# The end of a mixture-of-experts step: result rows of five token tiles gathered in two parts around the last three expert steps, and the last step's gate weights loaded ahead of its up weights

## Chip, cores and metric

One core of one Trainium2 chip. The metric is the device time of one execution in microseconds (us); the kernel before was timed three times. One further execution of it was profiled, and all rows below are from that one.

## What is computed

One decoder layer over 1024 prompt tokens and 32 sample tokens: a gated merge of latent attention and a spatial-gating MLP, then a mixture of 64 SwiGLU experts of which each token takes two, then a last norm. All data are float32. The change is in the end of the mixture and in the last norm:

```python
def run_block(args):
    xb, e = args
    h = jax.nn.silu(xb @ w_gate[e]) * (xb @ w_up[e])     # 1024 -> 256, twice
    return h @ w_down[e]                                  # 256 -> 1024
...
out = ys[pos] * w_sorted[:, None].astype(ys.dtype)
return jnp.zeros_like(xt).at[tok_sorted].add(out.astype(xt.dtype))
...
return x + y.reshape(b, s, d)          # channel_mixer
...
y_prompt = rmsnorm(xp, norm_f_g)       # over all 1024 + 32 rows
y_sample = rmsnorm(xs, norm_f_g)
```

So a token's output row is norm(x2 + g0 * y(first expert) + g1 * y(second expert)).

## The kernel before

Five engines run programs of their own and meet at semaphores. SP only issues DMAs; POOL issues the indirect ones. Tokens are in NT = 9 tiles of 128 rows (the last has 32). The core's memory is one tensor, `arena`, cut by hand into regions that are used again from stage to stage.

**Expert steps.** Experts are ranked by load. The 8 fullest get a step each (up to 128 rows), the others go in pairs (64 rows each), 36 steps (NST) in all; `expert_steps` writes the order out. The last three steps hold the six experts of ranks 54 to 59, all pairs. Rank r's expert number is a value that is loaded from `order_i`. Its three matrices of 1 MB go into one of four slots `w_e[0..3]`, each with a gate, an up and a down part; the last step uses slots 2 and 3, the one before it slots 0 and 1. In step n:

- POOL: `rows_in` gathers the step's token rows from `xt_rows` into `xg[n % 4]`, up to six steps ahead (L1755).
- PE: `turn_rows(n + 1)` (L1254), `turn_hidden(n - 1)` (L1273), `gate_up(n)` (L1266), `down(n - 1)` (L1285). `gate_up` waits for the gate and up weights of all its slots before its first matmul.
- ACT and DVE: copies between PSUM and `arena`; DVE's part of the result row is L2228, its share of the turned rows L2215.
- POOL: `rows_out` copies an index (L1749) and scatters the result rows into the DRAM tensor `y_rows` (L1763), at row 2 * token + choice. `scattered` waits until a scatter has landed.
- SP: `w_load(slot, e, (0, 1))` issues gate, up, gate, up for step n as soon as gate_up of the slot's last user is done; then `down_load` of step n - 1 (all L719).
- DVE has some 30 small pieces of other work, `overflow(k)`, one group per step, that find experts with too many rows. If there are any, a loop runs more steps after the last. In the profiled execution it runs none.

**The end.** When all scatters have landed POOL raises `moe_end`. Then SP loads each tile's 2 x 1024 values per token from `y_rows` (1 MB a tile, L786) into `y2[t]`, nine loads in order, the last three held back by the use of four semaphores. `y_rows` has the two rows of a token next to each other, so this is one plain copy for each tile. Tiles in PE_TILES = (2, 4, 6) are combined on PE: three matmuls for each half row, by the identity on x2 and by the diagonals `diag[t][c]` of the gates on the two result rows (L1319 to L1321). The six other tiles are combined on DVE by two instructions (L2278, L2279). ACT then squares and sums each row (L1588) and takes the root (L1589), DVE inverts it (L2270) and scales (L2272), and SP stores the row (L778). DVE and ACT take the tiles in order 0 to 8; in DVE's program the scale of tile t - 2 follows the combine of tile t.

Of the kernel before, what the change touches and what calls it, by code (L numbers as in the profile page):

```python
# [29 lines left out]
P = 128  # L30
# [34 lines left out]
PE_TILES = (2, 4, 6)  # L65
# [156 lines left out]
def build(nc, x_prompt, x_sample, cache_ckv, cache_krope, page_table, norm1_g, w_in, q_norm_g, kv_norm_g,  # L222
# [4 lines left out]
    with ExitStack() as ctx:  # L227
# [204 lines left out]
        o = [attn_base]  # L432
        y2 = [take(2 * D, o) for _ in range(NT)]
        fin = [x[:, 0:D] for x in y2]
        junk8 = take(D, o)
        stat8 = [take(2, o) for _ in range(NT)]
        diag = {t: [take(P, o) for _ in range(2)] for t in PE_TILES}
# [62 lines left out]
        moe_end = sem("experts_done")  # L500
        f_in = [sem(f"y_rows_in{i}") for i in range(4)]
# [35 lines left out]
        def group_moves(what, n, out):  # L537
# [27 lines left out]
            return [(qsr[half, :].rearrange("p (b h t) -> p h b t", b=NB, h=H), src) for half in (slice(0, DR), slice(DR, P))]  # L565

# [14 lines left out]
        def _(sp):  # L581
# [169 lines left out]
            for n, (_, mine) in enumerate(steps):  # L751
# [3 lines left out]
                for (_, slot, use), e in zip(mine, e_of):  # L755
                    sp.wait_ge(e_gu, step_of[slot, use - 1] + 1)
                    w_load(slot, e, (0, 1))
# [8 lines left out]
            with sp.If(total > 0):  # L766
                with sp.Fori(0, NOVP) as j:
                    with sp.If(total > 2 * j):
# [3 lines left out]
                        w_load(0, e0)  # L772
                        w_load(1, e1)
# [7 lines left out]
            yr = y_rows.rearrange("(n c) d -> n (c d)", c=2)  # L781
            for t in range(NT):
                r = rows_of(t)
                if t >= 4:
                    sp.wait_ge(f_in[t % 4], 16 * (t // 4))
                sp.dma_start(y2[t][0:r, :], yr[t * P:t * P + r, :]).then_inc(f_in[t % 4], 16)  # L786
                if t >= 6:
                    out_rows(sp, t - 6)
            for t in range(3, NT):
                out_rows(sp, t)  # L790
# [4 lines left out]
        def _(pe):  # L795
# [461 lines left out]
            def gate_up(n, u, mine):  # L1257

                pe.wait_ge(e_xe, 2 * n + 2)
                for _, slot, use in mine:  # L1260
                    pe.wait_ge(e_w[slot], 32 * use)
                for x in range(2):
                    for k in range(KD):
# [39 lines left out]
            with pe.If(total > 0):  # L1303
                with pe.Fori(0, NOVP) as j:
                    with pe.If(total > 2 * j):
                        extra = [(None, s, j + loads[s] + 1) for s in range(2)]
# [8 lines left out]
            for k, t in enumerate(PE_TILES):  # L1315
                pe.wait_ge(f_in[t % 4], 16 * (t // 4 + 1))
# [276 lines left out]
        def _(pool):  # L1593
# [177 lines left out]
            row_of = [row for row, _ in steps]  # L1771
            for n in range(4):
                rows_in(n, row_of[n], n)
# [3 lines left out]
            k = 6  # L1777
            for n in range(NST):
                if n >= 2:
# [26 lines left out]
            pool.sem_inc(moe_end, 1)  # L1806

# [3 lines left out]
        def _(dve):  # L1811
# [357 lines left out]
            def overflow(k):  # L2169
# [37 lines left out]
                elif k == 9:  # L2207
                    tt(g_sub, logits[:, :, 0:NG], g_top[:, :, 0:1].broadcast_to([P, NT, NG]), ALU.subtract)
                    step(tt(d_sub, e_top[:, :, 1], e_top[:, :, 0], ALU.subtract))
                    dve.sem_inc(r_sub, 1)  # L2210

# [49 lines left out]
            dve.wait_ge(moe_end, 1)  # L2261
# [3 lines left out]
            last.then_inc(r_dve, 1)  # L2265

# [7 lines left out]
            for t in range(NT):  # L2274
                r = rows_of(t)
                if t not in PE_TILES:
                    dve.wait_ge(f_in[t % 4], 16 * (t // 4 + 1))
# [37 lines left out]
```

## Time and profile before

| | us |
|---|---|
| median of 3 runs | 2040.82 |
| lowest, highest | 2031.3, 2046.83 |
| profiled execution | 2023.4 |
| its span, first to last instruction | 2021.6 |

The profiled execution lies below the three timed ones. PE is busy 1857.5 us of the span and its mean granted clock is 0.959 of full speed. The expert steps take the time from about 1460 to 1983, the end from there.

### The profile page before, as it was taken

The page shows a single profiled execution, that of the slowest core. Times are in us where ns is not written, and L with a number is a line of the kernel's source. Part 1 is how long each engine was busy: PE and PEld are TensorE (multiplying, and loading weights), DVE is VectorE, ACT ScalarE, POOL GpSimd, SP SyncE. Part 2 cuts the span into 40 slices and gives each one's busy share as a digit, 9 for nine tenths or more (in the row PEclk, how much of TensorE's full clock was granted, in tenths as well). Part 3 has the DMA queues.
Part 4 walks back from the last instruction along what each step waited for, and adds up shares of the span by engine and source line. Part 5 has one row for each costly group of instructions (what it writes and reads, how often), then busy time and mean ns, then how long its engine had stood idle before and what let it go on. Part 6 is the DMA issues. An engine that isn't in the chain of part 4 may idle for free. (4 is left out here: it accounts for less than half of the span.)

```text
span 2021.6 us, 26766 instructions
## 1 busy us (share of the span) xinstructions
PE 1857.5 (92%) x10622; PEld 1088.8 (54%) x10622; DVE 598.3 (30%) x1385; ACT 426.5 (21%) x904; POOL 301.4 (15%) x428
## 2 busy tenths in 40 slices
PE   7999999999999999998999998999598988888884
PEld 5644444444445656565666664555365555555551
DVE  3110000022203334333555554555322211111116
ACT  3211111100002223332444333222110011101103
POOL 1021221111100000000111112243412111111100
PEclk9999999999999999998999998999598889999997
DMA  7212211378820000024999996454599999999986
GB/s 232 107 68 80 75 36 70 116 261 284 276 86 1 1 1 1 1 63 128 292 305 292 294 304 224 148 185 162 192 400 421 420 416 416 415 402 403 407 342 260
DMA packets 105267, 433.86 MB, mean 215 GB/s; under 512 B 24208, under 2 KB 29808, under 8 KB 74384
## 3 DMA queue, kind: packets, MB, share of 16 engines
q1 hardware_dynamic: 84880, 331.06, 43.5%
q0 software_dynamic: 20160, 101.24, 15.0%
q8 instruction: 68, 1.11, 0.2%
q14 instruction: 31, 0.25, 0.0%
q10 hardware_dynamic: 128, 0.20, 0.0%
HBM read 389.22 MB, written 63.66 MB: 224 GB/s over the span
## 5 line engine op out<-in xcount | busy, mean ns | idle before, releaser
L838 PE MATMUL psum<-arena 128*128 128x512 f32 (+1 forms) x1280 | 527.3, 567 | 0.0
L838 PEld LDWEIGHTS psum<-arena 128*128 128x128 f32 x1280 | 239.6, 190 | 259.7 <-issue 235.7
L1266 PE MATMUL psum<-arena 128*64 128x256 f32 (+1 forms) x2048 | 284.4, 411 | 66.4 <-DMA arena<-in_w_up_dram 65.5
L1266 PEld LDWEIGHTS psum<-arena 128*64 128x64 f32 (+1 forms) x2048 | 204.8, 155 | 136.2 <-issue 79.2
L1285 PE MATMUL psum<-arena 128*64 128x512 f32 (+1 forms) x512 | 131.4, 595 | 0.7 <-DVE arena L2223 0.7
L1896 DVE COPY arena<-psum 128x512 f32<-128x512 f32 (+5 forms) x52 | 27.8, 545 | 346.9 <-PE psum L883 194.0
L1033 PEld LDWEIGHTS psum<-arena 128*128 128x128 f32 x1024 | 112.7, 141 | 30.0 <-issue 28.0
L1435 ACT ACTIVATE arena<-psum 128x512 f32<-128x512 f32 (+1 forms) x72 | 40.5, 562 | 412.6 <-PE psum L838 400.0
L1033 PE MATMUL psum<-arena 128*128 128x128 f32 x1024 | 126.6, 276 | 0.3 <-DVE arena L1950 0.3
L1163 PE MATMUL psum<-arena 128*128 128x512 f32 x256 | 113.4, 600 | 1.3 <-ACT arena L1484 1.3
L2219 DVE TENSOR_TENSOR arena<-arena,psum 128x256 f32<-128x256 f32 x36 | 15.2, 422 | 321.4 <-ACT arena L1549 321.4
L1449 ACT COPY arena<-psum 128x512 f32<-128x512 f32 x128 | 71.8, 587 | 172.6 <-PE psum L1033 172.6
L1763 POOL DMA_INDIRECT y_rows<-arena x36 | 40.7, 1132 | 411.8 <-DVE arena L2228 393.9
L1044 PE MATMUL psum<-arena 128*32 128x512 f32 (+1 forms) x768 | 95.6, 611 | 1.5 <-DVE arena L1950 1.5
L1950 DVE COPY arena<-psum 128x512 f32<-128x512 f32 x128 | 87.7, 691 | 28.1 <-PE psum L1033 24.8
L1549 ACT ACTIVATE arena<-psum 128x256 f32<-128x256 f32 x36 | 13.8, 384 | 337.2 <-PE psum L1266 337.2
L1918 DVE STREAM_TRANSPOSE arena<-arena 128x512 f32<-128x512 f32 x64 | 41.8, 692 | 133.3 <-DMA rope_turned<-arena 104.9
L1285 PEld LDWEIGHTS psum<-arena 128*64 128x64 f32 (+1 forms) x512 | 45.5, 142 | 66.2 <-issue 63.2
L1163 PEld LDWEIGHTS psum<-arena 128*128 128x128 f32 x256 | 48.3, 192 | 60.2 <-issue 60.1
L932 PE MATMUL psum<-arena 128*128 128x512 f32 (+3 forms) x192 | 72.8, 502 | 3.0 <-ACT arena L1379 3.0
L958 PE MATMUL psum<-arena 128*128 128x128 f32 x576 | 72.1, 277 | 3.2 <-ACT arena L1407 1.5
L958 PEld LDWEIGHTS psum<-arena 128*128 128x128 f32 x576 | 68.8, 193 | 11.5 <-issue 6.2
(307 smaller groups left out, 1949.8 us busy)
## 6 DMA issues: line engine op xcount, KB each, us to landing
arena<-in_w_gate_dram SPq DMA_DIRECT2D x64, 1024.0 KB, 13.3
arena<-in_w_up_dram SPq DMA_DIRECT2D x64, 1024.0 KB, 20.1
arena<-in_w_down_dram SPq DMA_DIRECT2D x64, 1024.0 KB, 21.8
arena<-in_w_in_dram SPq DMA_DIRECT2D x8, 2048.0 KB, 8.2
z_act<-arena SPq DMA_DIRECT2D x64, 256.0 KB
rope_turned<-arena SPq DMA_DIRECT2D x32, 512.0 KB
arena<-rope_turned SPq DMA_DIRECT2D x64, 256.0 KB
arena<-z_act SPq DMA_DIRECT2D x8, 2048.0 KB, 10.1
```

The lines of the kernel that those rows point to most:

```text
L838: last = mm(out[:, 0:w], xn_t[:, k, t * P:t * P + P], w_blk[n % 2][:, k, 0:w], start=(k == 0), stop=(k == KD - 1))
L932: mm(outs[h], q_pair[p % 2][:, h, t * P:t * P + P], kv_pair[p % 2][:, h, c0:c0 + w], start=True, stop=False)
L958: last = mm(out[:, DV * h:DV * h + DV], prob_t[h][:, j, :], v_pair[p % 2][:, j, DV * h:DV * h + DV], start=(j == 0), stop=(j == t))
L1033: last = tr(bank(u % 4)[:, P * kk:P * kk + P], ck[q][:, key_row(j, kk), P * c:P * c + P], ident)
L1044: last = mm(bank(5)[RS * j:RS * j + RS, :], q_now[:, c, :] if c < 2 else qr_now[half, :], ck_t[:, c, j, :] if c < 2 else rope[:, 4 * j:4 * ...
L1163: last = mm(bank(4 + half), m_t[:, k, :], w_o_sb[:, k, 512 * half:512 * half + 512], start=(k == 0), stop=(k == KD - 1))
L1266: last = mm(bank(2 + u)[rows, DE * x:DE * x + DE], xg_t[u][:, k, rows], w_e[slot][x][:, k, :], start=(k == 0), stop=(k == KD - 1))
L1285: last = mm(bank(5 + half)[rows, :], h_t[:, f, rows], w_e[slot][2][:, f, 512 * half:512 * half + 512], start=(f == 0), stop=(f == 1))
L1449: nc.scalar.copy(turned_at(u), bank(u % 4)).then_inc(kt_in[0], 1)
L1763: pool.indirect_dma_start(y_rows, bass.IndirectOffsetOnAxis(ap=idx_row[s], axis=0), yo[s], None, bounds_check=last_slot, oob_is_err=False) ...
L1918: last = V.transpose(kr_b[n % 2][:, c, :].rearrange("p (r k) -> p r k", r=PG), kr_raw[n % 2][:, :, 32 * c:32 * c + 32])
L1950: copy(turned_at(u), bank(u % 4)).then_inc(kt_in[1], 1)
```

## The change

The tiles are split into EARLY_TILES = (1, 3, 5, 6, 7) and PLAIN_TILES = (0, 2, 4, 8), and PE_TILES becomes (1, 3, 5, 7).

- For an early tile POOL gathers the rows of `y_rows` by index, 128 rows by 1024 for each of the two choices. It does so twice, ten indirect DMAs each time. The first time it takes the rows whose experts ran before the last three steps; these ten stand behind `rows_out` of the third-last step. The second time, after `moe_end`, it takes the remaining rows. An index out of bounds skips its row.
- DVE works the two index lists out, in `overflow(10)` to `overflow(14)`.
- `y2[1], y2[3], y2[5], y2[7]` take the places of the gate and up parts of slots 0 and 1, `y2[6]` that of `xg[2]` and `xg[3]`. The overflow loop uses slots 2 and 3 in place of 0 and 1.
- `y_rows` is filled with the input rows x before, by four DRAM to DRAM copies of 8.65 MB in all, behind SP's stores of the new cache rows.
- SP loads only the four plain tiles after `moe_end`.
- In the last step SP issues gate, gate, up, up, and `gate_up` waits for the gates (on the semaphore `x_loaded[0]`), and before its up half for the ups.
- The diagonals are computed before the wait for `moe_end`; there are eight in place of six.

```diff
-PE_TILES = (2, 4, 6)
+PE_TILES = (1, 3, 5, 7)
+EARLY_TILES = (1, 3, 5, 6, 7)
+PLAIN_TILES = (0, 2, 4, 8)
+LATE_STEPS = 3
...
+        def y_there(eng, t):
+
+            if t in PLAIN_TILES:
+                eng.wait_ge(f_in[PLAIN_TILES.index(t)], 16)
+            else:
+                k = EARLY_TILES.index(t)
+                eng.wait_ge(c_in[k % 4], cache_moves(k % 4) + 32 * (k // 4 + 1))
...
+            sp.wait_ge(fill_in, 16)
+            for c in range(2):
+                sp.dma_start(y_rows[TOK * c:TOK * c + SEQ, :], xp).then_inc(fill_in, 16)
+                sp.dma_start(y_rows[TOK * c + SEQ:TOK * c + TOK, :], xs).then_inc(fill_in, 16)
...
+            def gates_first(mine, e_of):
+
+                for x, done in ((0, x_loaded[0]), (1, None)):
+                    for (_, slot, use), e in zip(mine, e_of):
+                        if x == 0:
+                            sp.wait_ge(e_gu, step_of[slot, use - 1] + 1)
+                        sp.dma_start(w_e[slot][x].rearrange("p k n -> p (k n)"),
+                                     (w_gate, w_up)[x][0, bass.ds(e, 1)].rearrange("e (p k) n -> p (e k n)", p=P)
+                                     ).then_inc(done or e_w[slot], 16)
...
-            for t in range(NT):
-                r = rows_of(t)
-                if t >= 4:
-                    sp.wait_ge(f_in[t % 4], 16 * (t // 4))
-                sp.dma_start(y2[t][0:r, :], yr[t * P:t * P + r, :]).then_inc(f_in[t % 4], 16)
+            for k, t in enumerate(PLAIN_TILES):
+                r = rows_of(t)
+                sp.dma_start(y2[t][0:r, :], yr[t * P:t * P + r, :]).then_inc(f_in[k], 16)
...
+                split = isinstance(n, int) and n == NST - 1
+                if split:
+                    pe.wait_ge(x_loaded[0], 16 * ((NT + 1) // 2) + 32)
...
                 for x in range(2):
+                    if split and x == 1:
+                        for _, slot, use in mine:
+                            pe.wait_ge(e_w[slot], 32 * use - 16)
...
+            def y_gather(t, c, rows_i, done):
+                m = 2 * t + c
+                pool.indirect_dma_start(y2[t][:, D * c:D * c + D], None, y_rows, bass.IndirectOffsetOnAxis(ap=rows_i[:, m:m + 1], axis=0),
+                                        bounds_check=last_slot, oob_is_err=False).then_inc(done, 16)
+
+            n_late = NST - LATE_STEPS
             for n in range(NST):
-                if n >= 2:
+                if 2 <= n and n - 2 != n_late - 1:
                     scattered((n - 2) % 4, (n - 2) // 4 + 1)
                 rows_out(n % 4, n, row_of[n], k)
...
+                if n == n_late:
+                    scattered((n_late - 1) % 4, (n_late - 1) // 4 + 1)
+                    pool.wait_ge(e_gu, NST - 1)
+                    pool.wait_ge(e_xt, NST)
+                    pool.wait_ge(rows_split, 1)
+                    for t in EARLY_TILES:
+                        for c in range(2):
+                            y_gather(t, c, early_i, e_x[1])
...
             pool.sem_inc(moe_end, 1)
+            pool.wait_ge(e_x[1], 16 * len([n for n in range(NST) if n % 4 == 1]) + 32 * len(EARLY_TILES))
+            for k, t in enumerate(EARLY_TILES):
+                if k >= 4:
+                    pool.wait_ge(c_in[k % 4], cache_moves(k % 4) + 32 * (k // 4))
+                for c in range(2):
+                    y_gather(t, c, late_i, c_in[k % 4])
...
-            dve.wait_ge(moe_end, 1)
             for t in PE_TILES:
                 for c in range(2):
                     last = ts(diag[t][c], ident, gates[:, t, c:c + 1], None, ALU.mult)
             last.then_inc(r_dve, 1)
+            dve.wait_ge(moe_end, 1)
```

POOL's program before, from the scatter of step 32 (the first L1763 here) to the first instruction behind the steps:

```order
L1763 DMA y_rows<-arena 2112x1024
L1749 COPY arena<-arena 128x1
L1763 DMA y_rows<-arena 2112x1024
L1749 COPY arena<-arena 128x1
L1763 DMA y_rows<-arena 2112x1024
L1749 COPY arena<-arena 128x1
L1763 DMA y_rows<-arena 2112x1024
L1789 TENSOR_LOAD arena
```

The same stretch after; L1810 is the scatter and L1828 the gather from `y_rows`:

```order
L1810 DMA y_rows<-arena 2112x1024
L1796 COPY arena<-arena 128x1
L1810 DMA y_rows<-arena 2112x1024
L1828 DMA arena<-y_rows,arena 128x1024 x10
L1796 COPY arena<-arena 128x1
L1810 DMA y_rows<-arena 2112x1024
L1796 COPY arena<-arena 128x1
L1810 DMA y_rows<-arena 2112x1024
L1851 TENSOR_LOAD arena
```

Ten gathers now stand between the scatter of step 33 and that of step 34; ten more end POOL's program.

SP's program before, from the last step's gate and up weights to the last down weights:

```order
L719 DMA arena<-in_w_gate_dram 128x2048
L719 DMA arena<-in_w_up_dram 128x2048
L719 ISA
L719 DMA arena<-in_w_gate_dram 128x2048
L719 DMA arena<-in_w_up_dram 128x2048
L719 DMA arena<-in_w_down_dram 128x2048 x4
```

And after:

```order
L753 DMA arena<-in_w_gate_dram 128x2048
L753 ISA
L753 DMA arena<-in_w_gate_dram 128x2048
L753 DMA arena<-in_w_up_dram 128x2048 x2
L760 DMA arena<-in_w_down_dram 128x2048 x4
```

The second gate load has moved ahead of the first up load; the down loads stay where they were.

DVE's program before, from the first combine to the scale of tile 2 (L2278 and L2279 combine, L2270 and L2272 scale; a scale that reads psum is of a PE tile):

```order
L2278 SCALAR_TENSOR_TENSOR arena<-arena 128x1024
L2279 SCALAR_TENSOR_TENSOR arena<-arena 128x1024
L2278 SCALAR_TENSOR_TENSOR arena<-arena 128x1024
L2279 SCALAR_TENSOR_TENSOR arena<-arena 128x1024
L2270 RECIPROCAL arena<-arena 128x1
L2272 SCALAR_TENSOR_TENSOR arena<-arena 128x1024
L2278 SCALAR_TENSOR_TENSOR arena<-arena 128x1024
L2279 SCALAR_TENSOR_TENSOR arena<-arena 128x1024
L2270 RECIPROCAL arena<-arena 128x1
L2272 SCALAR_TENSOR_TENSOR arena<-arena 128x1024
L2270 RECIPROCAL arena<-arena 128x1
L2272 SCALAR_TENSOR_TENSOR arena<-psum,arena 128x1024
```

And after, from the first combine to the combine of tile 4:

```order
L2370 SCALAR_TENSOR_TENSOR arena<-arena 128x1024
L2371 SCALAR_TENSOR_TENSOR arena<-arena 128x1024
L2370 SCALAR_TENSOR_TENSOR arena<-arena 128x1024
L2371 SCALAR_TENSOR_TENSOR arena<-arena 128x1024
L2362 RECIPROCAL arena<-arena 128x1
L2364 SCALAR_TENSOR_TENSOR arena<-arena 128x1024
L2362 RECIPROCAL arena<-arena 128x1
L2364 SCALAR_TENSOR_TENSOR arena<-psum,arena 128x1024
L2370 SCALAR_TENSOR_TENSOR arena<-arena 128x1024
L2371 SCALAR_TENSOR_TENSOR arena<-arena 128x1024
```

Before, three combines and two scales of DVE's own tiles stand ahead of the first scale of a PE tile; now two combines and one scale do.

## Rows read from the trace of the kernel before

**Rows 1.** The chain that ended last, 1860 to 2022: start us, us, what.

```profile
1939.33 22.95 DMA arena<-in_w_up_dram
...
1962.41 7.15 PE psum L1266 x64
...
1974.11 3.68 PE psum L1285 x16
...
1979.40 2.38 DMA y_rows<-arena
...
1983.77 9.21 DMA arena<-y_rows
```

**Rows 2.** Stretches: us, busy of PE, PEld, DVE, ACT, POOL; PEclk, DMA share, GB/s.

```profile
1956.00:1960.00 4.00, 4.00 (x24) 1.52 (x20) 0.42 (x1) 0.97 (x2) 0.00 (x0) 1.00 0.45 188
1962.00:1967.00 5.00, 4.59 (x43) 3.66 (x45) 0.00 (x0) 0.00 (x0) 1.05 (x2) 1.00 0.97 394
1967.00:1979.00 12.00, 10.09 (x58) 4.42 (x54) 2.14 (x4) 3.20 (x6) 1.17 (x2) 1.00 0.07 25
```

**Rows 3.** SP's queue in order of time: start us, us, line, what.

```profile
1960.29 0.81 SPq L719 DMA_DIRECT2D arena<-in_w_down_dram  x2
...
1982.92 10.41 SPq L786 DMA_DIRECT2D arena<-y_rows  x7
```

**Rows 4.** DVE in order of time, the end; in brackets the idle time before.

```profile
1982.99 1.27 DVE L2264 TENSOR_SCALAR arena<-arena 128x128 f32<-128x128 f32 x6 [2.86 <-POOLq L1806]
1988.04 1.29 DVE L2278 SCALAR_TENSOR_TENSOR arena<-arena 128x1024 f32<-128x1024 f32 x1 [3.78 <-DMA arena<-y_rows]
...
1990.56 1.28 DVE L2278 SCALAR_TENSOR_TENSOR arena<-arena 128x1024 f32<-128x1024 f32 x1
...
2001.89 0.17 DVE L2270 RECIPROCAL arena<-arena 128x1 f32<-128x1 f32 x1 [2.40 <-ACT arena L1589]
...
2005.81 0.15 DVE L2270 RECIPROCAL arena<-arena 128x1 f32<-128x1 f32 x1
...
2007.20 0.16 DVE L2270 RECIPROCAL arena<-arena 128x1 f32<-128x1 f32 x1
...
2017.96 1.27 DVE L2272 SCALAR_TENSOR_TENSOR arena<-arena 32x1024 f32<-32x1024 f32 x1
```

**Rows 5.** PE in order of time, the three tiles that it combines.

```profile
1993.12 2.04 PE L1319 MATMUL psum<-arena 128*128 128x512 f32 x2 [15.35 <-DMA arena<-y_rows]
...
2000.22 1.02 PE L1319 MATMUL psum<-arena 128*128 128x512 f32 x2
...
2005.37 1.02 PE L1319 MATMUL psum<-arena 128*128 128x512 f32 x2
```

**Rows 6.** POOL in order of time: scatters back to back, then single ones.

```profile
1429.52 0.98 POOL L1711 DMA_INDIRECT slot_rows<-arena  x1 [0.30 <-issue]
1430.81 0.98 POOL L1711 DMA_INDIRECT slot_rows<-arena  x1 [0.30 <-issue]
...
1548.74 2.32 POOL L1763 DMA_INDIRECT y_rows<-arena  x1 [13.74 <-DVE arena L2228]
...
1560.60 1.03 POOL L1763 DMA_INDIRECT y_rows<-arena  x1 [7.31 <-DVE arena L2228]
...
1961.88 0.98 POOL L1763 DMA_INDIRECT y_rows<-arena  x1 [17.92 <-DVE arena L2228]
...
1974.62 0.98 POOL L1763 DMA_INDIRECT y_rows<-arena  x1 [11.56 <-DVE arena L2228]
```

**Rows 7.** DVE at the same times as the two single scatters of Rows 6.

```profile
1547.75 2.42 DVE L2187 TENSOR_TENSOR arena<-arena 128x2176 f32<-128x2176 f32 x1
...
1559.60 2.41 DVE L2189 TENSOR_REDUCE arena<-arena 128x34 f32<-128x2176 f32 x1
```

**Rows 8.** Landing of the row gathers (L1755) from 1850 on.

```profile
DMA to landing us min/median/max: 8.5/8.7/8.9
```

**Rows 9.** Busy time in the stretch behind SP's stores of the cache rows.

```profile
650.00:850.00 200.00, 194.37 (x950) 119.95 (x949) 74.60 (x197) 61.14 (x138) 0.00 (x0) 1.00 0.00 1
```

More of the change, by code:

```diff
@@ L430, in build @@
         fill = w_uk_t.rearrange("p h c -> p (h c)")[:, 0:2 * NE * CAPR // P]
-        o = [attn_base]
-        y2 = [take(2 * D, o) for _ in range(NT)]
+        slot_at = [attn_base + 6 * D * s for s in range(4)]
+        y_home = {1: slot_at[0], 3: slot_at[0] + 2 * D, 5: slot_at[1], 7: slot_at[1] + 2 * D, 6: attn_base + 26 * D,
+                  0: slot_at[0] + 4 * D, 2: slot_at[1] + 4 * D, 4: slot_at[2], 8: slot_at[2] + 2 * D}
+        y2 = [take(2 * D, [y_home[t]]) for t in range(NT)]
         fin = [x[:, 0:D] for x in y2]
+        o = [slot_at[3]]
         junk8 = take(D, o)
         stat8 = [take(2, o) for _ in range(NT)]
-        diag = {t: [take(P, o) for _ in range(2)] for t in PE_TILES}
+        assert o[0] <= attn_base + 4 * 6144
+        o = [gains_base + 4 * D]
+        kept_in = take(2 * NT * NE, o).rearrange("p (m e) -> p m e", e=NE)
+        limit, is_late, row_f, row_at = (take(2 * NT, o) for _ in range(4))
+        early_i, late_i = (take(2 * NT, o).bitcast(U32) for _ in range(2))
+        assert o[0] <= free[0]
+        diag = {t: [kept_in.rearrange("p m e -> p (m e)")[:, 2 * P * k + P * c:2 * P * k + P * c + P] for c in range(2)]
+                for k, t in enumerate(PE_TILES)}
         assert o[0] <= attn_base + 4 * 6144
@@ L754, in _ @@
                 e_of = [sp.value_load(order_i[0:1, r:r + 1], min_val=0, max_val=NE - 1) for r, _, _ in mine]
-                for (_, slot, use), e in zip(mine, e_of):
-                    sp.wait_ge(e_gu, step_of[slot, use - 1] + 1)
-                    w_load(slot, e, (0, 1))
+                if n == NST - 1:
+                    gates_first(mine, e_of)
+                else:
+                    for (_, slot, use), e in zip(mine, e_of):
+                        sp.wait_ge(e_gu, step_of[slot, use - 1] + 1)
+                        w_load(slot, e, (0, 1))
                 if e_last:
@@ L1305, in _ @@
                     with pe.If(total > 2 * j):
-                        extra = [(None, s, j + loads[s] + 1) for s in range(2)]
+                        extra = [(None, s, j + loads[s] + 1) for s in (2, 3)]
                         turn_rows(NST + j, 0, xg_used + 1 + j)
@@ L2210, in overflow @@
                     dve.sem_inc(r_sub, 1)
+                elif k == 10:
+                    late_e = [r for _, mine in steps[NST - LATE_STEPS:] for r, _, _ in mine]
+                    assert late_e == list(range(late_e[0], late_e[-1] + 1))
+                    cap, used, past = cnt[1], cnt[2], cnt[3]
+                    ts(cap, placed, float(NBIG), float(BLK), ALU.is_lt, ALU.mult)
+                    ts(used, placed, float(late_e[0]), None, ALU.is_lt)
+                    step(ts(past, placed, float(late_e[-1] + 1), None, ALU.is_ge))
+                    step(tt(used, used, past, ALU.add))
+                    step(stt(cap, cap, float(BLK), used, ALU.add, ALU.mult))
+                elif k == 11:
+                    step(tt(kept_in, iota.unsqueeze(1).broadcast_to([P, 2 * NT, NE]), wide(e_f.rearrange("p t c -> p (t c)"), NE), ALU.is_equal))
+                elif k == 12:
+                    step(tt(kept_in, kept_in, cnt[1].unsqueeze(1).broadcast_to([P, 2 * NT, NE]), ALU.mult))
+                elif k == 13:
+                    step(red(limit, kept_in, AX.X, ALU.add))
+                elif k == 14:
+                    tt(is_late, rk.rearrange("p t c -> p (t c)"), limit, ALU.is_ge)
+                    step(copy(row_f, ids_sb.rearrange("p (n c) -> p n c", c=2)[:, :, 0]))
+                    step(stt(row_at, is_late, float(1 << 20), row_f, ALU.mult, ALU.add))
+                    step(copy(early_i, row_at))
+                    step(ts(is_late, is_late, -float(1 << 20), float(1 << 20), ALU.mult, ALU.add))
+                    step(tt(row_at, is_late, row_f, ALU.add))
+                    step(copy(late_i, row_at))
+                    dve.sem_inc(rows_split, 1)
             def rows_t(n, u):
```

20 lines of the change are left out of this document (11 added, 9 removed).

## Prediction

> **What bounds the kernel now.** I read the chain that ended last first, since the change only touches the end. From 1860 to 1962 us the chain is the weight stream: the last up weights are issued at 1939.33 and land 22.95 us later, at 1962.28 [rows 1]. Behind that point come, one after another: the last gate_up (7.15 us), the down matmuls of step 34, the hidden rows, the last down matmuls at 1974.11, the last scatter at 1979.40 which lands in 2.38 us, `moe_end`, SP's first load of result rows at 1982.92 [rows 3], the third of these (tile 2, 9.21 us to landing), and then PE from 1993.12 [rows 5]. The view by stretches shows what the change wants to use: from 1967 to 1979 the DMA engines are 7% busy at 25 GB/s [rows 2], while after `moe_end` 8.65 MB must be read and 4.3 MB stored. All that the change can touch lies between 1960 and 2021.6, some 60 us or 3% of the span, and most of that is work that stays.
>
> The end itself runs at DVE's pace. The reader should see in [rows 4] one idle time of weight, 2.40 us before 2001.89: DVE waits for the first tile that PE combines. PE starts at 1993.12, takes 7.1 us for that tile and 5.15 us for the next [rows 5], and ACT needs another 1.5 us until DVE can scale at 2001.89. From there DVE never stands still: seven scales and three combines. A scale costs 1.39 us (2005.81 to 2007.20), a combine 2.5 us (1988.04 to 1990.56). 7 x 1.39 + 3 x 2.5 = 17.2, so the sum gives 2019.1; the row says 2017.96 + 1.27 = 2019.2. The last store then takes 2.4 us to the end of the span. So before, **end = S + 8.8 + 17.2 + 2.4**, where S is PE's first combining matmul.
>
> **Gates ahead of ups.** Four loads of 1 MB come in the order gate, gate, up, up; at some 0.4 MB/us the two ups are 5 us of the stream, so the gates are there near 1957. PE had finished the down matmuls of step 33 by 1960.29, when SP issues the down loads that wait for them [rows 3], and stood still until 1962.41 but for two transposes. Now it can begin at about 1960.7; the gate half takes 3.6 us, and at 1964.3 the ups (1962.28) are there. Gain for the last down matmuls: 1.7 us, so the last result rows are in memory at about 1976.9 in place of 1978.6.
>
> **Ten early gathers on POOL.** The scatter of step 33 ends at 1962.86 [rows 6]. Back-to-back indirect DMAs are issued every 1.29 us [rows 6], so ten take 12.9 us, from 1963.1 to 1976.0. Queued behind them on POOL are the scatters of steps 34 and 35. An index copy and its wait cost 1.0 us each time (a scatter follows 1.0 us behind the end of the last DMA), so scatter 34 goes at 1977.0 (before 1974.62) and scatter 35 at 1979.0 (before 1979.40). POOL's queue is now what ends last there, not PE: of the 1.7 us of the gates 0.4 are left. Two things can take them back. The eight diagonals (8 x 0.21 = 1.7 us of DVE, from [rows 4]) now run at just that time; before they filled a wait. And the early gathers bring up to 5.2 MB into the DMA queue that the scatters use: at the 394 GB/s of [rows 2], with the 1.5 MB of down weights that are left at 1963.4, they drain by about 1980. Scatter 35 lands in 2.4 us if the queue is empty, in up to 5 us if not. I take `moe_end` at the same time as before, with bounds of -1 and +4 us. The last down weights, landed by 1967 before, share the DMA engines with the gathers; they would have to be 5 us late to be missed at 1972.4.
>
> **What is loaded after `moe_end`.** SP issues 3.25 MB in four loads, not 8.65 MB. Tile 0 comes as before (1988.04), tile 2 as the second load at about 1990.5, so DVE has no wait in front. For tile 1 POOL must issue two gathers, the second at 1984.2. Few rows are in them, so only the latency counts: 2.4 us as the last scatter [rows 1], 8.7 us as the row gathers under the weight stream [rows 8]. With SP's loads in flight until about 1991 I take 6.3 us: **S = 1990.5**, between 1986.6 and 1992.9; before it was 1993.12. The other four early tiles follow at 2.6 us each, by 1994.5 issued, ahead of PE's 5.15 us a tile.
>
> The latency under load is weighed against a rule: the Trainium skill (DMA: Bandwidth & Descriptors, Queues, rings and completion order) says that a DMA engine changes between queues only at packets of about 9 to 17 descriptors. That would explain the 8.7 us of [rows 8] and speaks for a value near it here; by it the sum would be 2 us higher.
>
> **DVE and PE at the end.** DVE has five combines in place of six and nine scales as before. Tile 1 is now PE's, and its scale is third in DVE's order, behind two combines and one scale, which are done by 1994.5. So DVE waits from there until S + 8.8 = 1999.3; then eight scales and three combines are left: 11.1 + 7.5 = 18.6. **End = S + 8.8 + 18.6 + 2.4 = S + 29.8 = 2020.3.** PE's four tiles end at S + 7.1 + 3 x 5.15 = S + 22.6, and their last scale stands at S + 24.7 in DVE's order: just covered. So PE starting 2.6 us earlier is paid back by one more scale behind the wait (1.4 us). Against the 2021.6 us of the span this is -1.3 us.
>
> **Edits with no cost.** The fill of `y_rows` (8.65 MB read and written) is issued near 605 us; from 650 to 850 the DMA engines move 1 GB/s [rows 9], and 17.3 MB need 88 us at half of the 394 GB/s of [rows 2]. The index work on DVE is two instructions of 1152 columns, a reduction and some fifteen small ones, some 7 us over five steps; DVE has pieces of 2.4 us in such steps already [rows 7], and between its copy of a result row and its next due copy lie some 7 us of gate_up. If that cover were gone it would be 7 us at most.
>
> **Rivals.** (1) *The late gathers come quickly.* S = 1986.6 and `moe_end` 1 us early: 2016.4 - 1 = about 2015.5, -6 us. For it: few bytes. Against: the 8.7 us of [rows 8].
>
> (2) *DVE keeps POOL from issuing the late gathers.* At 1548.74 a scatter took 2.32 us: it ended 0.9 us after a DVE TENSOR_TENSOR on two `arena` operands (1547.75 + 2.42); under a TENSOR_REDUCE of the same length the next took 1.03 us [rows 6, 7]. DVE's instructions at the end read two `arena` operands too, back to back from 1988 on. Four of the ten gathers are out by then. If each of the other six must wait for the end of a DVE instruction and 0.9 us more, they come every 2.5 us, the last at 2003, in time for PE. If POOL gets its turn only when DVE is idle, DVE's wait for tile 1 (4.8 us) serves three, and DVE then stands still at tile 6 for the rest: three issues and a landing, 3 x 1.29 + 3 = 7 us. That gives 2027, 6 us slower than before. It decides from the point at which late gathers take over 2.3 us each. The Trainium skill (SBUF — State Buffer, Who interferes with whom) says that a DVE instruction with two inputs in this memory contends with a GpSimd instruction that reads it, and that a reduction doesn't; the trace agrees.
>
> (3) *The early gathers hold up the last scatters and down weights.* 5.2 MB in one queue ahead of them, with DMA engines that finish unevenly: before, the stream was down to 45% from 1956 to 1960 [rows 2] while the last up weights still took until 1962.28. Such 4 us on `moe_end` give 2024.3, with a late tile 1 as well 2026.5: 3 to 5 us slower than before.
>
> **The numbers.** Forecast, within 3 us of 2020.3: 0.40. Rival 1: 0.20. Rival 2: 0.20. Rival 3: 0.20. The profiled execution took 2023.4 us, its span 2021.6; the median of three is 17 us higher, and the three differ by 15 us, which nothing in the end of the kernel explains. I carry the difference over: 2040.8 - 1.3 = 2039.5. The cases span -6 to +6 us; medians of so few runs can differ by some 7 us by themselves. Together the range is 2029 to 2050. No case reaches 1% (20 us, about what a measurement of this kernel can tell from no change): 0.03 faster, 0.93 same, 0.04 slower.
>
> **What would show it.** PE's last gate_up starts near 1960.7 and the scatter of step 35 is issued near 1979.0, behind ten gathers 1.29 us apart; `moe_end` is unchanged; PE's first combining matmul comes 7 to 8 us after SP's first load; DVE has one wait of 4 to 5 us before the first scale that reads PSUM. I am wrong if scatter 35 lands after 1985, if late gathers take over 1.3 us, or if a stretch before 1960 us gets longer.

## The result: half a per cent slower, and the profile after

| | before | after |
|---|---|---|
| median, us (20 runs each, same chip) | 2030.4 | 2040.01 |
| lowest, highest | 2024.11, 2046.83 | 2032.17, 2048.87 |
| ratio after/before, 95% interval | | 1.0046 [1.0033, 1.0059] |
| span of the profiled execution | 2021.6 | 2030.3 |

The change costs some 9 us. That is inside the 1% that I called "same", but its sign is not the one I forecast (-1.3 us). The absolute time, 2040.01, fell on my 2039.5 by luck, for a reason that has nothing to do with the change: the median of the three runs that I started from lies 10 us above the median of all twenty. From 2030.4 the same sum gives 2029.1, and the range of 2029 to 2050 is right only by this.

How to compare two profiles of this kernel needs one remark. The expert steps end at another time in each execution: SP's issue of the last two down loads, which falls on DVE's copy of the result row of step 33 (1960.29 in [rows 3]), is seen anywhere from 1956.9 to 1975.4 us in the twelve profiles. All that the change touches at the end comes behind that moment, so I count from it ("+13.8" is 13.8 us behind it).

The changed kernel was profiled twice, and the first profile holds a disturbance that none of the ten later profiles shows: at 1970 and at 1976 it has waits of ACT (12.80 us) and DVE (4.92 us) that end 4 to 6 us behind the matmuls they wait for, with a releaser that the trace doesn't know. Its cause stays open, and I read the second profile (`e5_again`, the same kernel, span 2037.1) for the time up to `moe_end`. Behind `moe_end` the two agree within 0.7 us.

PE of the second profile, which answers to the first rows of [rows 1] and to [rows 5]; columns start, us, what, and in brackets the idle time before it and what ended it:

```profile
1968.13 7.17 PE L1313 MATMUL psum<-arena 128*64 128x256 f32 x64
1975.89 3.66 PE L1332 MATMUL psum<-arena 128*64 128x512 f32 x16 [0.58 <-DMA arena<-in_w_down_dram]
1979.48 0.51 PE L1320 MATMUL psum<-arena 128*128 128x128 f32 x2
1982.85 5.35 PE L1332 MATMUL psum<-arena 128*64 128x512 f32 x16 [2.87 <-DMA arena<-in_w_down_dram]
2007.26 2.05 PE L1366 MATMUL psum<-arena 128*128 128x512 f32 x2 [19.05 <-DMA arena<-y_rows,arena]
```

The zero point of this profile is 1967.80. gate_up of the last step starts at +0.3 (before +2.1, [rows 1]). But the last down matmuls start at +15.05 instead of +13.82, because now they wait for their weights, and they take 5.35 us instead of 3.68. The stretches say why they take longer:

```profile
1968.00:1976.00 8.00, 7.42 (x68) 4.68 (x69) 1.07 (x3) 0.38 (x1) 5.09 (x6) 1.00 0.92 338
1976.00:1980.00 4.00, 3.98 (x18) 1.43 (x17) 0.60 (x2) 0.59 (x1) 3.08 (x4) 1.00 1.00 389
1980.00:1984.00 4.00, 1.15 (x6) 0.65 (x8) 0.61 (x2) 0.00 (x0) 2.98 (x4) 0.96 1.02 380
1984.00:1988.00 4.00, 4.00 (x13) 1.12 (x9) 0.00 (x0) 1.87 (x2) 1.22 (x2) 0.61 1.01 408
```

The columns are, as in [rows 2], the us of the stretch, the busy time of PE, PEld, DVE, ACT and POOL, the granted clock, the DMA share and GB/s. PE was busy for 1.15 of the 4 us before 1984, and the granted clock of the next stretch is 0.61: PE ran most of it at 1.2 GHz. The DMA engines, 7% busy at this place before, are full until 1988.

The chain that ended last has the two landings in question, where [rows 1] had 2.38 for the scatter:

```profile
1968.23 14.38 DMA arena<-in_w_down_dram
...
1982.85 5.37 PE psum L1332 x16
...
1989.85 4.49 DMA y_rows<-arena
```

POOL's and SP's queues, answering to [rows 6] and [rows 3]:

```profile
1969.39 0.98 POOL L1810 DMA_INDIRECT y_rows<-arena  x1 [17.08 <-DVE arena L2320]
1970.67 1.04 POOL L1828 DMA_INDIRECT arena<-y_rows,arena  x1 [0.30 <-issue]
...
1982.41 0.99 POOL L1828 DMA_INDIRECT arena<-y_rows,arena  x1 [0.31 <-issue]
1983.41 0.19 POOL L1796 COPY arena<-arena 128x1 uint32<-128x1 uint32 x1
1984.45 1.03 POOL L1810 DMA_INDIRECT y_rows<-arena  x1 [0.85 <-POOL arena L1796]
...
1989.85 1.01 POOL L1810 DMA_INDIRECT y_rows<-arena  x1 [4.17 <-DVE arena L2320]
1996.23 1.03 POOL L1828 DMA_INDIRECT arena<-y_rows,arena  x1 [5.38 <-issue]
1997.57 1.01 POOL L1828 DMA_INDIRECT arena<-y_rows,arena  x1 [0.30 <-issue]
```

```profile
1967.80 0.81 SPq L760 DMA_DIRECT2D arena<-in_w_down_dram  x2
1995.48 2.03 SPq L828 DMA_DIRECT2D arena<-y_rows  x4
```

SP's first load of result rows stands at +27.7; before it was at +22.6. The second late gather of tile 1 is issued at 1997.57, and PE can start on that tile at 2007.26, 9.7 us later. DVE pays for it, answering to the 2.40 us of [rows 4]:

```profile
2000.42 1.28 DVE L2370 SCALAR_TENSOR_TENSOR arena<-arena 128x1024 f32<-128x1024 f32 x1 [8.18 <-DMA arena<-y_rows]
...
2006.05 1.29 DVE L2364 SCALAR_TENSOR_TENSOR arena<-arena 128x1024 f32<-128x1024 f32 x1
2016.02 0.16 DVE L2362 RECIPROCAL arena<-arena 128x1 f32<-128x1 f32 x1 [8.69 <-ACT arena L1636]
...
2033.47 1.27 DVE L2364 SCALAR_TENSOR_TENSOR arena<-arena 32x1024 f32<-32x1024 f32 x1
```

The first profile has 9.50 us at the place of the 8.69.

The account from the zero point, before against the second profile of after: last down matmuls 1.2 us later and 1.7 us longer, the landing of the last scatter 2.1 us longer, together 5.0 us up to SP's first load; from there to the end 41.6 instead of 38.7 us, 2.9 more. That makes 8.0 us, beside the 6.9 and 9.3 us that the two timed ratios of this kernel amount to.

### The profile page after: what moved, and what is told of

It reads as the page before. It is cut to its first block and busy times, and to the rows that moved or that the text cites. A ratio compares the mean times of both kernels' runs of the same rounds, so it can differ in the third digit from the quotient of the medians.

```text
span 2030.3 us, 26831 instructions
## 1 busy us (share of the span) xinstructions
PE 1864.8 (92%) x10634; PEld 1091.4 (54%) x10634; DVE 604.8 (30%) x1400; ACT 426.6 (21%) x904; POOL 322.3 (16%) x448
## 5 line engine op out<-in xcount | busy, mean ns | idle before, releaser
L1964 DVE COPY arena<-psum 128x512 f32<-128x512 f32 (+5 forms) x52 | 27.8, 545 | 348.1 <-PE psum L923 194.0
L1073 PEld LDWEIGHTS psum<-arena 128*128 128x128 f32 x1024 | 112.7, 141 | 29.5 <-issue 27.3
L1496 ACT COPY arena<-psum 128x512 f32<-128x512 f32 x128 | 71.8, 587 | 171.1 <-PE psum L1073 171.1
L1810 POOL DMA_INDIRECT y_rows<-arena x36 | 41.0, 1140 | 404.2 <-DVE arena L2320 386.6
L1596 ACT ACTIVATE arena<-psum 128x256 f32<-128x256 f32 x36 | 13.8, 384 | 338.3 <-PE psum L1313 325.5
L998 PEld LDWEIGHTS psum<-arena 128*128 128x128 f32 x576 | 68.8, 193 | 11.5 <-issue 6.4
## 6 DMA issues: line engine op xcount, KB each, us to landing
arena<-in_w_up_dram SPq DMA_DIRECT2D x64, 1024.0 KB, 20.1
arena<-z_act SPq DMA_DIRECT2D x8, 2048.0 KB, 10.2
```

Of the source, the lines that this page charges most:

```text
L998: last = mm(out[:, DV * h:DV * h + DV], prob_t[h][:, j, :], v_pair[p % 2][:, j, DV * h:DV * h + DV], start=(j == 0), stop=(j == t))
L1073: last = tr(bank(u % 4)[:, P * kk:P * kk + P], ck[q][:, key_row(j, kk), P * c:P * c + P], ident)
L1496: nc.scalar.copy(turned_at(u), bank(u % 4)).then_inc(kt_in[0], 1)
L1810: pool.indirect_dma_start(y_rows, bass.IndirectOffsetOnAxis(ap=idx_row[s], axis=0), yo[s], None, bounds_check=last_slot, oob_is_err=False) ...
```

## The experiments

Ten more kernels ran, one of them the changed kernel again, each timed against the kernel before on its chip. The table has them all, with before and after; every column is in us from the zero point, read from each kernel's timeline as above, except "load to end" and "load to PE", which are differences. "Down" is PE's start of the last down matmuls, "row" DVE's copy of the last result row, "load" SP's first load of result rows, "PE" its first combining matmul.

| kernel | down | row | load | load to PE | load to end | end | ratio [95%] |
|---|---|---|---|---|---|---|---|
| before | 13.8 | 17.5 | 22.6 | 10.2 | 38.7 | 61.3 | |
| after, first profile | 18.5 | 24.4 | 29.5 | 11.5 | 42.3 | 71.8 | 1.0046 [1.0033, 1.0059] |
| e5_again | 15.1 | 20.4 | 27.7 | 11.8 | 41.6 | 69.3 | 1.0034 [1.0008, 1.0060] |
| e1_gates_only | 13.5 | 17.2 | 22.6 | 9.9 | 38.2 | 60.7 | 0.9993 [0.9974, 1.0012] |
| e2_no_gates | 15.7 | 19.4 | 27.8 | 12.1 | 41.7 | 69.5 | 1.0058 [1.0034, 1.0082] |
| e3_empty_first | 13.4 | 17.1 | 22.3 | 14.9 | 45.8 | 68.0 | 1.0025 [1.0006, 1.0044] |
| e4_sp_loads | 13.4 | 17.1 | 26.1 | 11.9 | 42.4 | 68.5 | 1.0018 [0.9996, 1.0040] |
| e6_two_tiles | 14.7 | 20.1 | 25.3 | 11.3 | 41.0 | 66.2 | 1.0025 [1.0000, 1.0050] |
| e7_hold_plain | 14.9 | 20.3 | 27.7 | 8.0 | 38.1 | 65.8 | 1.0014 [0.9989, 1.0039] |
| e8_plain_pe4 | 13.4 | 17.1 | 22.2 | 7.6 | 37.2 | 59.4 | 0.9992 [0.9967, 1.0018] |
| e9_two_after_down | 13.3 | 17.0 | 26.4 | 11.5 | 42.2 | 68.6 | 1.0037 [1.0016, 1.0058] |
| e10_fill_index | 14.3 | 18.0 | 23.1 | 10.0 | 38.1 | 61.2 | 0.9987 [0.9962, 1.0012] |

The intervals reach 3 to 5 us to each side, so the timed ratios tell the groups apart (near 1.000, or up to 1.006; the intervals of e4_sp_loads, e6_two_tiles and e7_hold_plain reach from 1.000 to losses of 0.4 or 0.5% and decide nothing by themselves) and the profiles tell where the time is. A profile is one execution of each kernel, so differences of a few tenths of a us between rows of the table say little.

**The gate order alone.** The kernel before, with `gates_first` for the last step and the wait of `gate_up` split as in the change:

```diff
-                for (_, slot, use), e in zip(mine, e_of):
-                    sp.wait_ge(e_gu, step_of[slot, use - 1] + 1)
-                    w_load(slot, e, (0, 1))
+                if n == NST - 1:
+                    gates_first(mine, e_of)
+                else:
+                    ...
```

> The kernel before with the last step's gate weights ahead of its up weights and nothing else. In the changed kernel PE's last gate_up was dispatched 1.7 us earlier, but its semaphore came 4.15 us after the modelled end of its last matmul, and that of the down matmuls of step 34 5.9 us after. Theory T (the first ten gathers cause this, by their traffic): here the semaphores come within 0.03 us of the ends, the last DVE copy of a result row is 1.5 to 2 us earlier, ratio about 0.999. Rival G (the split of gate_up causes it): the lag of 4 to 6 us is here too and the ratio is 1.001 to 1.003.

```profile
1963.61 7.17 PE L1286 MATMUL psum<-arena 128*64 128x256 f32 x64
1971.88 3.66 PE L1305 MATMUL psum<-arena 128*64 128x512 f32 x16 [1.09 <-DMA arena<-in_w_down_dram]
1975.46 0.51 PE L1293 MATMUL psum<-arena 128*128 128x128 f32 x2
1976.83 3.66 PE L1305 MATMUL psum<-arena 128*64 128x512 f32 x16 [0.86 <-DVE arena L2243]
```

This is PE with its zero point at 1963.28. gate_up starts 1.8 us sooner, as forecast, and then PE stands 1.09 us before the down matmuls of step 34, whose weights follow the ups in the same stream. At the last row 0.3 us of the 1.8 are left, where I had expected 1.5 to 2. The timed ratio shows neither gain nor loss.

**The change without the gate order**, so the counterpart:

```diff
-                if n == NST - 1:
+                if False:
                     gates_first(mine, e_of)
...
-                split = isinstance(n, int) and n == NST - 1
+                split = False
```

> The changed kernel with the last step's weights in the old order (gate, up, gate, up) and one wait for all. T: the lag of 4 to 6 us between the end of PE's last gate_up and its semaphore stays, ratio 1.004 to 1.006 to before, as the whole change. G: no lag, moe_end near its old distance from the last steps, ratio 1.000 to 1.002.

1.0058 holds the whole loss, and its interval lies clear of that of the gate order alone, so the gathers and what goes with them are the cause. The lag that I expected here is absent. Its last down matmuls start at +15.7 and its load comes at +27.8, near those of the whole change, but in this profile by another way:

```profile
1970.52 8.72 PE L1313 MATMUL psum<-arena 128*64 128x256 f32 x64 [1.99 <-DMA arena<-in_w_up_dram]
...
1983.79 3.66 PE L1332 MATMUL psum<-arena 128*64 128x512 f32 x16 [0.68 <-DVE arena L2315]
```

The last down matmuls do not wait for their weights and run at full clock. What is late is gate_up: after 1.99 us of idle time it took 8.72 us, at a granted clock of 0.50 from 1970.5 to 1972, where that of before took 7.15 us after 1.72. The gathers need not be the reason: in e10_fill_index, which has none, the same gate_up took 7.16 us after 2.18 us of idle time, and one of an earlier step 8.76 us after 1.96. The second down load landed 14.5 us after its issue, at about +14.9; with a gate_up of 7.15 us the last down matmuls would have been ready near +14.1 and would have met the miss of the whole change. What the gathers surely cost this profile is the last scatter: issued at 1989.10, it took 5.68 us to landing.

**The first ten gathers without bytes.** All rows are counted as late, so the early gathers are issued and skip every row; the late ones fetch all:

```diff
-                    tt(is_late, rk.rearrange("p t c -> p (t c)"), limit, ALU.is_ge)
+                    ts(is_late, limit, 0.0, 1.0, ALU.mult, ALU.add)
```

> The changed kernel with every row counted as late: the first ten gathers are issued but skip all rows, the ten after moe_end move all 5.2 MB. The output stays whole. T: no lag on PE, moe_end 6 to 7 us earlier against the last steps than in the changed kernel; but the end is longer, since tile 1 and the rest now bring all bytes after moe_end: some 5 us. Rival P (POOL's issuing of ten indirect DMAs is what delays PE's signals, not the bytes): the lag of 4 to 6 us stays.

```profile
1970.29 3.66 PE L1332 MATMUL psum<-arena 128*64 128x512 f32 x16 [0.94 <-DMA arena<-in_w_down_dram]
1994.08 2.04 PE L1366 MATMUL psum<-arena 128*128 128x512 f32 x2 [20.14 <-DMA arena<-y_rows,arena]
```

With ten instructions on POOL but no bytes, the load is back at +22.3. So it is the bytes, not POOL's time, that hold up `moe_end`. The price shows behind it, where 5.2 MB more must come: PE starts 14.9 us after SP's load.

**The same bytes by SP's queue.** In place of the first ten gathers SP issues ten plain loads of 512 KB behind the last down loads. They read another tensor, so this kernel leaves out the right early rows of the five tiles and its output is not the layer's; it serves for the time alone:

```diff
+            for t in EARLY_TILES:
+                for c in range(2):
+                    sp.dma_start(y2[t][:, D * c:D * c + D], z_act[t * P:t * P + P, D * c:D * c + D]).then_inc(x_loaded[1], 16)
```

> The changed kernel with the first ten gathers replaced by ten plain 512 KB loads on SP's queue, at the same time and into the same places, but from another tensor (z_act). The early rows of five tiles are therefore not the computed ones. T, if any traffic of this size does it: the lag on PE stays at 4 to 6 us. If it is the gather on POOL's queue alone (its descriptors or its sharing with the down weights): no lag, and moe_end 5 to 7 us earlier against the last steps than in the changed kernel, ratio to before 0.998 to 1.002.

```profile
1960.01 0.81 SPq L760 DMA_DIRECT2D arena<-in_w_down_dram  x2
1960.91 10.84 SPq L810 DMA_DIRECT2D arena<-z_act  x10
1986.11 2.02 SPq L833 DMA_DIRECT2D arena<-y_rows  x4
```

Behind the down weights in one queue the bytes no longer delay them (+13.4). The scatter of step 35, issued at 1978.68 (+18.7), still needs 7.4 us until SP's load at 1986.11; before that was 3.5 us [rows 1, 3]. So there are two separate costs: the down weights, and the last scatter. I had expected either the lag of the first profile or a `moe_end` 5 to 7 us earlier than in it; there is no lag, and the load is 3.4 us earlier.

**The changed kernel again**, for a second profile and more runs:

> The changed kernel once more, to see whether the lag between the ends of PE's last gate_up and its semaphore (4.15 us in its profile, and 5.8 us for the last down matmuls of step 34) belongs to the kernel. If it does: again 4 to 6 us, and the last DVE copy of a result row some 24 us behind that of step 33. If it was a disturbance of one execution: semaphores within 0.03 us, that distance near 17.5 us, and the end of the span some 67 to 70 us behind the copy of step 33. Ratio in both cases 1.004 to 1.006.

The lag of the first profile wasn't there, the loss was (1.0034). Its lines stand above.

**Two tiles gathered early** in place of five, four gathers instead of ten; SP loads seven tiles:

```diff
-EARLY_TILES = (1, 3, 5, 6, 7)
-PLAIN_TILES = (0, 2, 4, 8)
+EARLY_TILES = (1, 3)
+PLAIN_TILES = (0, 2, 4, 5, 6, 7, 8)
```

> The changed kernel with only tiles 1 and 3 gathered in two parts (four gathers early, four late) and seven tiles loaded plainly. If the gathered bytes hold up the last scatter in proportion (3.3 us for 5.2 MB in the profile of the kernel without the gate order), SP's first load comes 3.5 to 4.5 us behind the last scatter in place of 6.8; SP's loads then last longer, so tile 1's late rows land no sooner than 9 us after their issue. Ratio 1.001 to 1.004.

```profile
1976.30 0.51 PE L1323 MATMUL psum<-arena 128*128 128x128 f32 x2
1979.73 5.35 PE L1335 MATMUL psum<-arena 128*64 128x512 f32 x16 [2.92 <-DMA arena<-in_w_down_dram]
```

Four gathers make the down weights nearly as late as ten do, and PE comes back to the same 5.35 us. The last scatter, at 1986.73, lands in 2.38 us as before; the 2 MB are through by then, with the DMA engines 9% busy:

```profile
1979.70:1985.00 5.30, 5.27 (x16) 1.72 (x16) 0.00 (x0) 2.23 (x4) 0.00 (x0) 0.68 0.09 26
```

So from four gathers to ten the first cost doesn't grow, and the second does.

**Two of SP's four loads held back.** SP waits for tile 1's late rows before it issues tiles 4 and 8, 1.25 of its 3.25 MB:

```diff
             for k, t in enumerate(PLAIN_TILES):
                 r = rows_of(t)
+                if k == 2:
+                    y_there(sp, 1)
```

> The changed kernel with SP holding back its loads of tiles 4 and 8 until tile 1's late rows have landed. Theory Q (the few late rows land 9 to 10 us after their issue because SP's 3.25 MB are queued in front of them in every DMA engine): with half of these bytes ahead PE's first combining matmul comes 8 to 9.5 us behind SP's first load in place of 11.5 to 12, and the end of the span is 2 to 3 us nearer to SP's first load. Rival (a gather costs 9 us whatever is queued): 11.5 to 12 us stay, and the end gets worse, since tiles 4 and 8 come late. Ratio by Q 0.001 to 0.0015 below that of the changed kernel.

```profile
1990.62 8.69 SPq L830 DMA_DIRECT2D arena<-y_rows  x4
```

```profile
1998.63 2.04 PE L1368 MATMUL psum<-arena 128*128 128x512 f32 x2 [15.43 <-DMA arena<-y_rows,arena]
```

The 8.69 us of SP are its four issues with the wait in their middle. Tile 1's second late gather lands in 5.77 us, where e5_again has 9.55. PE starts 8.0 us after the first load, not 11.8, and the time from load to end falls from 41.6 to 38.1 us. What made tile 1 late is what SP had in flight. This is nearly the tail that I had forecast (37.4), and it beats that of before by only 0.6 us.

**Plain loads for all tiles**, no gathers, no fill: the kernel before with the gate order, the diagonals ahead of `moe_end` and PE_TILES = (1, 3, 5, 7):

```diff
-PE_TILES = (2, 4, 6)
+PE_TILES = (1, 3, 5, 7)
...
-            dve.wait_ge(moe_end, 1)
             for t in PE_TILES:
...
+            dve.wait_ge(moe_end, 1)
```

> The kernel before with only the cheap parts of the change: gates ahead of ups in the last step, diagonals computed ahead of moe_end, PE's tiles (1, 3, 5, 7); all nine tiles loaded plainly after moe_end, no indirect gathers, no fill. Expected: last DVE copy 0.3 to 0.6 us earlier, PE's first combining matmul 7.7 us behind SP's first load (10.2 before), then 29.8 to 31 us to the end: 37.5 to 38.7 us from SP's first load to the end, before 38.7. Ratio 0.9985 to 0.9995.

```profile
1997.61 2.10 SPq L800 DMA_DIRECT2D arena<-y_rows  x4
```

```profile
2005.20 2.05 PE L1340 MATMUL psum<-arena 128*128 128x512 f32 x2 [12.71 <-DMA arena<-y_rows]
```

The best tail of all, though 8.65 MB are read behind `moe_end`: tile 1 comes second in SP's queue, PE starts on it 7.6 us after the first load, and from load to end it is 37.2 us. The whole is 1.9 us shorter from the zero point than before; timed, 0.9992 can't be told from no change. It is the version I would keep of these, and it does not beat the kernel before by anything that these runs can measure.

**Two tiles, gathered behind the down weights.** As e6_two_tiles, and POOL waits for the last step's down weights before its four early gathers:

```diff
+                    for _, slot, use in steps[NST - 1][1]:
+                        pool.wait_ge(e_wd[slot], 16 * use)
```

> As e6 (only tiles 1 and 3 in two parts), but POOL waits until the last step's down weights have landed before its four early gathers. Theory D (the early gathers make the last down weights late on the DMA engine that is furthest behind, and PE stands and then runs at the lower clock): the last down matmuls start at 13.4 to 13.8 us behind the DVE copy of step 33 in place of 14.74, and the last DVE copy comes at 17.1 us in place of 20.1. The scatter of step 34 is then late (near 20 us) and that of step 35 near 21 us, so SP's first load gains no more than 1 us. Rival (what delays the last down matmuls is something else, such as POOL's work): 14.7 and 20.1 us stay. Ratio 1.001 to 1.004.

```profile
1971.75 12.41 DMA arena<-in_w_down_dram
...
1993.06 3.53 DMA y_rows<-arena
```

```profile
1984.97 1.03 POOL L1831 DMA_INDIRECT arena<-y_rows,arena  x1 [11.08 <-DMA arena<-in_w_down_dram]
...
1993.06 1.00 POOL L1813 DMA_INDIRECT y_rows<-arena  x1 [0.85 <-POOL arena L1799]
```

The down weights are in time (+13.3, 3.66 us of matmuls). But now POOL's own queue is the bound: both scatters stand behind gathers that begin 13.6 us after the zero point, and the load comes at +26.4, later than in e6_two_tiles.

**Fill and index work alone**, added to the kernel before and not used:

```diff
+            for c in range(2):
+                sp.dma_start(y_rows[TOK * c:TOK * c + SEQ, :], xp).then_inc(fill_in, 16)
+                sp.dma_start(y_rows[TOK * c + SEQ:TOK * c + TOK, :], xs).then_inc(fill_in, 16)
```

> The kernel before with only the fill of y_rows and DVE's index work in the expert steps added; the indices are used by nothing. If both are hidden as forecast: ratio 0.999 to 1.001 and the expert steps' pace unchanged. Rival: part of the 0.46% is lost there, by the 17.3 MB of traffic or by late DVE copies in five steps: ratio 1.001 to 1.003.

The stretch from 600 to 650 us, of this kernel and then of before:

```profile
600.00:650.00 50.00, 47.88 (x177) 27.55 (x177) 15.22 (x41) 13.05 (x32) 4.23 (x8) 1.00 0.59 193
```

```profile
600.00:650.00 50.00, 47.87 (x176) 27.72 (x175) 15.23 (x41) 13.66 (x33) 4.54 (x8) 1.00 0.09 27
```

The DMA engines are 59% busy in place of 9%, and PE's busy time is the same. The ratio is 0.9987: no cost shows, and by the interval it is 0.12% at most.

## Why the prediction was wrong

**The step that failed first is "I take `moe_end` at the same time as before".** SP's first load came 5.0 us later, outside my bound of +4, and scatter 35 landed at +26.5, behind the 1985 (+24.7) that I had named as a sign of being wrong. Under it lies one false reading: "the last down weights, landed by 1967 before". I had taken that from the DMA share, which is 97% until 1967 and 7% behind it [rows 2]. But a share of 7% is as much as one of 16 engines at work all the time, and a load has landed only when its last part has. Over the loads issued from 1960.2 on, the trace of before gives the median from issue to landing:

```profile
arena<-in_w_down_dram SPq DMA_DIRECT2D x2, 1024.0 KB, 10.4
```

So they landed near 1971, and against the 1972.4 at which I wanted them the cover was 1.3 us, not 5. In e9_two_after_down, where nothing is queued beside them, the second takes 12.41 us and is still just in time; with gathers beside it it takes 14.38, and is missed. Over the eleven profiles that record it the second load lands in 10.4 to 12.9 us where no gathered bytes lie beside it (seven profiles) and in 14.1 to 14.5 where they do (e2_no_gates, e5_again, e6_two_tiles, e7_hold_plain). e6_two_tiles, e3_empty_first, e4_sp_loads and e9_two_after_down show it from four sides: late with four gathers as with ten, in time without bytes, with the bytes queued behind, or with the gathers issued after. The miss also costs clock: PE's pause before the last down matmuls is followed by 1.7 us more of matmuls. That term was nowhere in my sum. The other part, the last scatter behind gathered bytes, I had named ("in up to 5 us if not") and priced inside the bound; it took 4.49 us. This is rival 3, which I gave 0.20. Against before I had priced it at +3 us, and at +5 with a late tile 1 as well; the latter is what came, and it cost 8.0.

**The step that failed second is S, the start of PE**, with the 6.3 us for tile 1's late rows. They took 9.7 us, outside the 2.4 to 8.7 of my bounds, and the gathers were issued 0.8 us later behind SP's load than I had reckoned: 11.8 us from SP's load to PE, not 7.6. The near row, 8.7 us under the weight stream [rows 8], was the better guide than the middle that I took. e7_hold_plain shows the cause: with two of SP's four loads held back it is 8.0. The Trainium skill (DMA: Bandwidth & Descriptors, Queues, rings and completion order) has a DMA engine change between queues only at whole packets, and by it I had put the sum 2 us higher. The trace agrees in sign, with 3.4 us more than the 6.3 that I took; no run here shows the packets themselves.

Together: 5.05 (load) + 4.2 (S) is 9.3 us more than forecast, and -1.3 + 9.3 gives the 8.0 of the profile.

**The gates were sized wrongly.** gate_up starts when I said, but I let its 1.7 us run through to the last down matmuls; the weights of step 34 stand between, and 0.3 us came out (e1_gates_only). In the sum this hardly mattered, since I had counted only 0.4 us of it.

**What held.** Behind S the time is 29.8 us in the second profile, as forecast (29.6 to 30.8 in the others with PE tiles 1, 3, 5 and 7): DVE's order and its 1.39 and 2.5 us pieces carry over. The gathers come 1.30 us apart and scatter 34 at +16.6 (forecast 1977.0, or +16.7). Fill and index work show no cost (e10_fill_index). The DVE wait came where I put it, but with 8.7 to 9.5 us in place of 4 to 5, since it is the same late tile 1.

**Rival 1** (late gathers quick) didn't happen. **Rival 2** (DVE keeps POOL from issuing) did, at a small price. POOL and DVE of e3_empty_first, where it shows best:

```profile
1987.84 1.60 POOL L1828 DMA_INDIRECT arena<-y_rows,arena  x1 [0.30 <-issue]
```

```profile
1987.29 1.28 DVE L2370 SCALAR_TENSOR_TENSOR arena<-arena 128x1024 f32<-128x1024 f32 x1 [0.62 <-DMA arena<-y_rows]
```

The gather starts inside DVE's instruction and ends 0.87 us after its end, 0.61 us later than the usual 0.99 us would have it. In the eight profiles with late gathers none that starts inside such an instruction ends sooner than 0.86 us after it. Seven were made clearly longer, to between 1.08 and 1.83 us, and each of these ends 0.86 or 0.87 us after DVE's instruction; the 2.32 us scatter of [rows 6] ends 0.89 us after its TENSOR_TENSOR. This is read from the traces; no run took DVE's instruction away. The price is small because DVE's instruction is short (1.28 us) and POOL gets its turn behind each one, even when the next follows at once. After that most gathers start just before one ends, as in the first profile of after, 0.13 us before:

```profile
1995.31 1.00 POOL L1828 DMA_INDIRECT arena<-y_rows,arena  x1 [0.30 <-issue]
```

```profile
1994.16 1.28 DVE L2371 SCALAR_TENSOR_TENSOR arena<-arena 128x1024 f32<-128x1024 f32 x1
1995.36 1.28 DVE L2370 SCALAR_TENSOR_TENSOR arena<-arena 128x1024 f32<-128x1024 f32 x1
```

So they keep their pace, under the 2.3 us from which that rival decides. And it is not what makes tile 1 late: in e5_again both of its gathers are issued before DVE's first combine (1998.58 against 2000.42).

Left open: the lag of the first profile, and what decides whether PE's clock falls after a pause of about 2 us.

## What to carry to other kernels

A low DMA share doesn't say that a load has landed: read the time from issue to landing of the very load that the next step needs before calling it covered. A gap in DMA traffic just ahead of a barrier is poor room for early loads when the last weights and the last scatter still have to come through it, and a PE pause of about 3 us there is paid again in a lower clock, 1.7 us on the next 16 matmuls in three profiles of three. And where a tile is wanted early after a barrier, its place in one queue (second, 7.6 us from the first load to PE) was worth more than having most of its bytes already (11.8 us): the few that were left took 9.7 us beside the bytes of the other queue.

## What the runs showed that I had not expected

- The time to landing of the same 1 MB load, nothing gathered beside it, differs between executions by 2.5 us (10.4 us in before, 12.41 in e9_two_after_down, 12.9 in e1_gates_only), which is more than the cover it had.
- After idle times of 2.87, 2.92 and 3.06 us (e5_again, e6_two_tiles, e7_hold_plain) PE's next 16 matmuls took 5.35 us, at a granted clock of 0.61 or 0.68 in stretches that cover them; after idle times of 0.58 to 1.09 us they took 3.66. Around 2 us it goes either way: gate_up took 8.72 us after 1.99 (e2_no_gates) and 8.76 after 1.96, but 7.16 after 2.18 (both e10_fill_index). This swing of 1.6 us comes with and without gathers, and is more than the gate order gained.
- An indirect DMA that POOL starts inside a DVE instruction on two `arena` operands ends 0.86 to 0.89 us after that instruction, for SCALAR_TENSOR_TENSOR (up to 1.83 us in place of 0.99, e4_sp_loads) as for TENSOR_TENSOR (2.32 us, [rows 6, 7]). The Trainium skill (SBUF — State Buffer, Who interferes with whom) has contention between a DVE instruction with two inputs there and a GpSimd instruction that reads it; the traces agree.
- An indirect DMA that skips all its rows takes as long to issue as a full one: 0.99 us, 1.30 us apart, in e3_empty_first.
